# Moving the down biases to a late place and adding the last expert's last down row straight to the tokens' sums

## The reference

```python
def moe_ffn(h, w_router, b_router, w_gu, b_gu, w_down, b_down):
    logits = (h @ w_router).astype(jnp.float32) + b_router.astype(jnp.float32)
    top_v, top_i = lax.top_k(logits, TOP_K)
    gates = jax.nn.softmax(top_v, axis=-1)
    ...
    def expert_block(args):
        e, toks, gw = args
        xb = h[toks]
        gu = xb @ w_gu[e] + b_gu[e]
        gate = jnp.minimum(gu[:, :D_FF], SWIGLU_LIMIT)
        up = jnp.clip(gu[:, D_FF:], -SWIGLU_LIMIT, SWIGLU_LIMIT)
        act = gate * jax.nn.sigmoid(gate * SWIGLU_ALPHA) * (up + 1.0)
        y = act @ w_down[e] + b_down[e]
        return (y * gw[:, None]).astype(h.dtype)
    ...
    return jax.ops.segment_sum(y.reshape(n_slots, -1), slot_tok, num_segments=T)
```

## Time and profile before

| | |
|---|---|
| median of 3 runs | 989.25 us |
| profiled execution | 988.7 us |
| its span, first to last instruction | 986.9 us |
| PE busy | 946.6 us (96%) |
| DVE, ACT busy | 202.9 us (21%), 127.7 us (13%) |
| moved by DMA | 418.27 MB, mean 424 GB/s |

### The profile page before, as it was taken

The page is one execution under the profiler, slowest core; times in us unless marked ns, Lnnn a source line. Parts: engine busy times, 40 slices in busy tenths (PEclk is TensorE's granted clock), DMA queues, the critical chain, the costliest instruction groups (busy, mean ns, idle before and its releaser), DMA issues.

```text
span 986.9 us, 11112 instructions
## 1 busy us (share of the span) xinstructions
PE 946.6 (96%) x4508; PEld 382.4 (39%) x4508; DVE 202.9 (21%) x610; ACT 127.7 (13%) x346; POOL 14.0 (1%) x9
## 2 busy tenths in 40 slices
PE   9999999999999899898989989889989999999997
PEld 5545433333333334333333333333333333333432
DVE  4645121212111121210112121011212112111121
ACT  2433111011110111010011101001101110011101
POOL 0031000000000000000000000000000000000000
PEclk9999999999999999999999999999999999999999
DMA  9999999999999999999999999999999999999996
GB/s 374 426 423 398 412 429 434 432 430 428 432 431 429 436 430 430 434 432 429 434 433 426 437 432 428 437 430 429 436 429 431 432 429 430 431 433 430 422 422 272
DMA packets 23869, 418.27 MB, mean 424 GB/s; under 512 B 2912, under 2 KB 3296, under 8 KB 8224
## 3 DMA queue, kind: packets, MB, share of 16 engines
q1 hardware_dynamic: 23408, 417.20, 99.2%
q10 hardware_dynamic: 432, 0.66, 0.2%
HBM read 416.80 MB, written 1.05 MB: 423 GB/s over the span
## 4 chain that ended last, share of the span: by engine, by line
PE 63%; DMA 36%; DVE 1%; issue 0%; ACT 0%; SPq 0%; DVEq 0%
DMA ring<-w_gu_dram 33%; PE ps L1237 29%; PE ps L1342 14%; PE ps L1205 4%; PE ps L1189 4%; DMA ring<-w_down_dram 3%; PE ps L1066 3%; PE ps L997 2%; PE ps L1004 1%; PE ps L1293 1%; PE ps L1301 1%; PE ps L1013 0%; PE ps L1039 0%; PE ps L1058 0%; PE ps L1046 0%
## 5 line engine op out<-in xcount | busy, mean ns | idle before, releaser
L1237 PE MATMUL ps<-ring,passing 128*64 128x512 f32 x1008 | 229.1, 604 | 14.8 <-DMA ring<-w_gu_dram 14.8
L1237 PE MATMUL ps<-ring,PR 128*64 128x512 f32 x976 | 224.5, 608 | 16.4 <-DMA ring<-w_gu_dram 16.2
L1342 PE MATMUL ps<-ring,PT 128*64 128x512 f32 x984 | 218.3, 595 | 0.5 <-DMA ring<-w_down_dram 0.5
L952 DVE TENSOR_SCALAR xw<-ps 128x256 f32<-128x256 f32 x64 | 27.2, 425 | 650.0 <-PE ps L1237 650.0
L1237 PEld LDWEIGHTS ps<-ring,passing 128*64 128x64 f32 x1008 | 76.8, 139 | 158.3 <-issue 143.8
L1237 PEld LDWEIGHTS ps<-ring,PR 128*64 128x64 f32 x976 | 74.9, 140 | 157.0 <-issue 145.4
L1342 PEld LDWEIGHTS ps<-ring,PT 128*64 128x64 f32 x984 | 68.1, 137 | 129.6 <-issue 127.5
L652 ACT ACTIVATE xw<-xw 128x256 f32<-128x256 f32 x64 | 26.6, 416 | 484.5 <-DVE xw L952 484.5
L1205 PE MATMUL ps<-PT 64*128 64x512 f32 x248 | 69.7, 640 | 0.0
L1189 PEld LDWEIGHTS ps<-qk,X 128*128 128x128 f32 x512 | 59.6, 191 | 18.8 <-issue 18.8
L1189 PE MATMUL ps<-qk,X 128*128 128x128 f32 x512 | 65.7, 281 | 0.0
(11 more groups left out here) (198 smaller groups left out, 374.6 us busy)
## 6 DMA issues: line engine op xcount, KB each, us to landing
ring<-w_gu_dram SPq DMA_DIRECT2D x48, 4096.0 KB, 28.2
ring<-w_down_dram SPq DMA_DIRECT2D x25, 4096.0 KB, 29.7
ring<-w_gu_dram SPq DMA_DIRECT2D x14, 2048.0 KB, 14.2
ring<-w_gu_dram SPq DMA_DIRECT2D x6, 3072.0 KB, 23.2
ring<-w_down_dram SPq DMA_DIRECT2D x5, 2048.0 KB, 23.1
ring<-w_gu_dram SPq DMA_DIRECT2D x9, 1024.0 KB, 9.6
ring<-w_down_dram SPq DMA_DIRECT2D x8, 1024.0 KB, 25.9
ring<-w_down_dram SPq DMA_DIRECT2D x2, 3584.0 KB, 27.6
```

The source lines that it names most:

```text
L952: nc.vector.tensor_scalar(gb[:, b, :], gu[:, b, 0, :], LIMIT, None, ALU.min).then_inc(g_ready, 1)
L1237: last = mm(ps[64 * j:64 * j + 64, GU + b, :], lhs, halves[j][:, 512 * b:512 * b + 512], start=start, stop=stop)
L1342: last = mm(ps[64 * j:64 * j + 64, bank, :], at[:, k, 64 * (c - GU_PIECES):64 * (c - GU_PIECES) + 64], rows[:, 512 * j:512 * j + 512], sta ...
```

## The change

1. **Biases late, half a row early.** Where `b_down` was loaded, the first half (512 of 1024 columns) of the first down row of expert 26 is now loaded into the same place, `PT[:, 1, 512:1024]`. The ring load of that expert's down weights leaves it out. `b_down` is stored twice over on the host side (128 partitions in place of 64) and is loaded into `spare`, whose weights expert 24 has used by then, in SyncE's order behind the first gate-up pair of expert 26. The four bias products stand behind expert 27 in place of expert 3.
2. **The last down row.** Down row 7 of expert 31 no longer goes through `ye`. PE makes `a_tokens` ahead of time: the activations that belong to this row, turned to the tokens with the gates (128 features x 256 tokens). ScalarE copies it to SBUF. When row 7 is there, four direct products over 128 rows add `a_tokens` times the row to the sums. Between them stand the four 64-row products that bring rows 0 to 6 to the tokens.
3. **Order at the end.** `to_tokens(0)` of expert 30 stands ahead of rows 0 and 1, `to_tokens(1)` ahead of row 2.
4. **Stores.** Four stores of 256 KB, each issued after its copy (SyncE for the first half of a tile, ScalarE for the second), in place of one of 512 KB and two of 256 KB.

```diff
-        "b_down": np.asarray(inputs["b_down"]).reshape(NE, 2, DM // 2).transpose(1, 0, 2).reshape(2 * NE, DM // 2),
+        "b_down": np.tile(np.asarray(inputs["b_down"]).reshape(NE, 2, DM // 2).transpose(1, 0, 2).reshape(2 * NE, DM // 2), (2, 1)),
...
-        aT_last, ye_last = gb.rearrange("p b (f s) -> p (b f) s", f=2), sg.rearrange("p b n -> p (b n)")
+        aT_last, ye_last = extra[:, 0, 0:512].rearrange("p (f s) -> p f s", f=4), sg.rearrange("p b n -> p (b n)")
+        a_tokens = extra[:, 1, 0:T * P]
...
-        down_ahead = [mixP[:, :, :].rearrange("p g s -> p (g s)"), xT[:, FF:2 * FF]]
+        down_ahead = [mixP[:, :, :].rearrange("p g s -> p (g s)"), xT[:, FF:2 * FF], PT[:, 1, 512:1024]]
+        DOWN_AHEAD = (DM, DM, DM // 2)
+        bdn = spare[:, 0:512]
...
             sp.wait_ge(half_used, 1)
-            sp.dma_start(bdn, b_down).then_inc(ld_bdn, 16)
+            load_down_ahead(2)
...
-                load_pair(s, NE - 3 * TURN, 2 * FF if gu_ahead else DM if s in (TP + GU_PIECES, TP + PIECES + GU_PIECES) else 0)
+                u, c = (s - TP) // PIECES, (s - TP) % PIECES
+                down_part = DOWN_AHEAD[u] if s > TP and u < len(DOWN_AHEAD) and c == GU_PIECES else 0
+                load_pair(s, NE - 3 * TURN, 2 * FF if gu_ahead else down_part)
+                if s == TP + 2 * PIECES:
+                    sp.dma_start(bdn, b_down).then_inc(ld_bdn, 16)
...
-            sp.wait_ge(out_v, 1)
-            sp.wait_ge(out_a, 1)
-            sp.dma_start(out_t[0], X[:, 0, :]).then_inc(stored, 16)
-            sp.wait_ge(out_v, T)
-            sp.dma_start(out_t[1][:, 0:512], X[:, 1, 0:512]).then_inc(stored, 16)
-            sp.wait_ge(stored, 16 * 3)
+            for t in range(T):
+                sp.wait_ge(out_v, t + 1)
+                sp.dma_start(out_t[t][:, 0:512], X[:, t, 0:512]).then_inc(stored, 16)
+            sp.wait_ge(stored, 16 * 2 * T)
...
-            down_out(NE - 1, 0, GU + 1, ye_last)
+            act.wait_ge(a_tokens_psum, 1)
+            nc.scalar.copy(a_tokens, ps[:, GAT, T * P:2 * T * P]).then_inc(a_tokens_sb, 1)
+            act.wait_ge(last_rows, 1)
+            nc.scalar.copy(ye_last, ps[:, GU + 1, :]).then_inc(y_sb, 1)
...
                 act.wait_ge(acc_final, 2 * t + 2)
                 nc.scalar.copy(X[:, t, 512:1024], ps[:, ACC[t] + 1, :]).then_inc(out_a, 1)
-            act.wait_ge(out_a, T)
-            act.dma_start(out_t[T - 1][:, 512:1024], X[:, T - 1, 512:1024]).then_inc(stored, 16)
+                act.wait_ge(out_a, t + 1)
+                act.dma_start(out_t[t][:, 512:1024], X[:, t, 512:1024]).then_inc(stored, 16)
...
-                dve.wait_ge(acc_final, 2 * t + 2)
+                dve.wait_ge(acc_final, 2 * t + 1)
                 nc.vector.tensor_copy(X[:, t, 0:512], ps[:, ACC[t], :]).then_inc(out_v, 1)
...
-            down_last(aT_last, GU + 1, range(2))
-            pe.wait_ge(gt_sb, NE - 1)
+            pe.wait_ge(gt_sb, NE)
+            mm(ps[:, GAT, T * P:2 * T * P], gb[64:128, 1, P:2 * P], GT_last[64:128].rearrange("p t s -> p (t s)"), start=True, stop=True, skip_group_check=True).then_inc(a_tokens_psum, 1)
             pe.wait_ge(y_sb, NE - 1)
             to_tokens(0)
-            down_last(aT_last, GU + 1, range(2, KC))
+            down_last(aT_last, GU + 1, range(2))
             to_tokens(1)
-            pe.wait_ge(gt_sb, NE)
-            pe.wait_ge(y_sb, NE)
+            down_last(aT_last, GU + 1, range(2, KC - 1))
+            pe.wait_ge(a_tokens_sb, 1)
+            row = last_row()
             for t in range(T):
-                for last in to_tokens(t, GT_last, ye_last):
-                    last.then_inc(acc_final, 1)
+                for j in range(2):
+                    direct = mm(ps[:, ACC[t] + j, :], a_tokens[:, t * P:(t + 1) * P], row[:, 512 * j:512 * j + 512], start=False, stop=True, skip_group_check=True)
+                    if t == T - 1 and j == 1:
+                        direct.then_inc(pieces_used, 1)
+                    if t == 0 and j == 0:
+                        pe.wait_ge(y_sb, NE)
+                    mm(ps[:, ACC[t] + j, :], GT_last[64 * j:64 * j + 64, t, :], ye_last[64 * j:64 * j + 64, :], start=False, stop=True, skip_group_check=True).then_inc(acc_final, 1)
```

More of the change, by code:

```diff
@@ L206, in layer_kernel @@
         pooled = PT[:, 1, :].rearrange("p (g s) -> p g s", g=NG)
-        bdn = PT[0:2 * NE, 1, 512:1024]
         tmp = PR[:, 1, :]
@@ L308, in layer_kernel @@
         ld_wout, ld_bdn, ld_bgu = sem("ld_wout"), sem("ld_bdn"), sem("ld_bgu")
-        ld_down_ahead = [sem(f"ld_down_ahead{u}") for u in range(2)]
+        ld_down_ahead = [sem(f"ld_down_ahead{u}") for u in range(3)]
         landed = [sem(f"landed{c}") for c in range(RING // 2)]
@@ L342, in layer_kernel @@
         more_done = sem("more_done")
+        a_tokens_psum, a_tokens_sb, last_rows = sem("a_tokens_psum"), sem("a_tokens_sb"), sem("last_rows")
         acc_final, out_a, out_v = sem("acc_final"), sem("out_a"), sem("out_v")
@@ L416, in load_down_ahead @@
             def load_down_ahead(u):
-                sp.dma_start(down_ahead[u], w_dn_k[:, NE - 2 * TURN + u, 0:DM]).then_inc(ld_down_ahead[u], 16)
+                sp.dma_start(down_ahead[u], w_dn_k[:, NE - 2 * TURN + u, 0:DOWN_AHEAD[u]]).then_inc(ld_down_ahead[u], 16)
             def load_aside(k):
@@ L1331, in down @@
                         first_ahead = early in (0, 1) and c == GU_PIECES
+                        half_ahead = early == 2 and c == GU_PIECES and k == 0
                         rows = piece(c, 4)[:, k, :]
@@ L1340, in down @@
                             wait_landed(c)
+                        if half_ahead:
+                            pe.wait_ge(ld_down_ahead[2], 16)
                         for j in range(2):
                             last = mm(ps[64 * j:64 * j + 64, bank, :], at[:, k, 64 * (c - GU_PIECES):64 * (c - GU_PIECES) + 64],
-                                      rows[:, 512 * j:512 * j + 512],
-                                      start=c == GU_PIECES and k == 0, stop=c == PIECES - 1 and k == 3)
-                        if k == 3:
+                                      down_ahead[2] if half_ahead and j == 0 else rows[:, 512 * j:512 * j + 512],
+                                      start=c == GU_PIECES and k == 0, stop=c == PIECES - 1 and k == (2 if step == "last" else 3))
+                        if step == "last" and c == PIECES - 1 and k == 2:
+                            last.then_inc(last_rows, 1)
+                        elif k == 3:
                             last.then_inc(pieces_used, 1)
@@ L1348, in down, with last_row @@
                             last.then_inc(row_used, 1)
+                def last_row():
+                    pe.wait_ge(landed_end[u, GU_PIECES, KC - 1], 16)
+                    return piece(PIECES - 1, 4)[:, 3, :]
                 if last_two:
-                    return gate_up, between, turn_round, turn_gates, down
+                    return gate_up, between, turn_round, turn_gates, down, last_row
                 if step == "more":
@@ L1372, in _ @@
                 expert(0, u, "first" if u == 0 else None)
+            with pe.Fori(1, TURNS - 2) as r:
+                for u in range(TURN):
+                    expert(r, u)
+            for u in range(TURN):
+                expert(TURNS - 2, u, early=u)
             pe.wait_ge(ld_bdn, 16)
@@ L1378, in _ @@
                     mm(ps[:, ACC[t] + c, :], GdT[c * NE:(c + 1) * NE, t, :], bdn[c * NE:(c + 1) * NE, :], start=False, stop=True, skip_group_check=True)
-            with pe.Fori(1, TURNS - 2) as r:
-                for u in range(TURN):
-                    expert(r, u)
-            for u in range(TURN):
-                expert(TURNS - 2, u, early=u)
             for u in range(TURN - 2):
                 expert(TURNS - 1, u, early=TURN + u)
-            gate_up, between, _, _, down = expert(TURNS - 1, TURN - 2, "last but one")
+            gate_up, between, _, _, down, _ = expert(TURNS - 1, TURN - 2, "last but one")
             gate_up()
             between()
-            gate_up, _, turn_round, turn_gates, down_last = expert(TURNS - 1, TURN - 1, "last")
+            gate_up, _, turn_round, turn_gates, down_last, last_row = expert(TURNS - 1, TURN - 1, "last")
             gate_up()
```

## The result

The change makes the kernel slower: 993.01 us (991.93 to 993.93, 6 runs) against 989.25 us (988.49 to 990.02, 6 runs) in the same comparison, a ratio of 1.0039 (95% interval 1.0028 to 1.0049). A second comparison of the two gave 1.0031 (1.0020 to 1.0041), with a median of 992.24. The forecast was 994.1 us in a range of 991.8 to 996.2. The profiled execution took 992.06 us with a span of 990.3 us, 3.4 more than the 986.9 of the earlier trace rows; the forecast was 5.0 more.

The account below looks back on a forecast made before the run. Stream and PE bound the end, after 978.5 us PE alone. Row 6 ending at 979.8, plus 6.9 and 1.4, gives 988.1; copy and store end at 991.9, 5.0 over the span: 994.25, stated as 994.1, range 991.8 to 996.2.

Parts of the forecast that it names:

- What bounds the kernel: End of kernel: bound twice, by the weight stream and by PE, and after 978.5 us by PE alone.
- Part 3: PE's tail after row 6: eight products at 0.86 each, 6.9 us, plus eight changes of shape, 1.4 us.
- Rival B: PE's tail: lone 64-row products run in the shadow of full ones, so not slower, 989.3 us; chance 0.06.
- rival A: Late biases and PE's tail: no lateness from biases, changes of shape free, 992.0 us; chance 0.11.
- Part 1: Late biases: about 0.4 us on the stream, and PE 0.9 late at the end of expert 30's down.
- the recovery: PE's waits after 875 us, before the one at 970.9: 0.9 + 0.5 = 1.4 us absorbs late bias products.
- The late 0.05: Weight stream, late: biases come in and 256 KB of weights leave a 4 MB transfer, costing 0.05 us.
- The early 0.33: Weight stream, early: 256 KB of weights replace 128 KB of biases, costing 0.33 us; lower bound for the stream 0.
- The 0.27: to_tokens(0) at the end: 0.27 us from the copy's end to the product, so it starts at 971.5.
- Part 4: Stores at the end: the last store goes alone and lands 2.5 us after issue, bounds 1.9 and 3.0.
- C: Stream and tail: short loads slow the stream by 1.5 us, changes cost 0.34 each, 996.1 us; chance 0.07.
- D: Last down row: still waited for, landing at 979.7; result within 0.4 of the forecast and counted there.

Follow-up runs that it names:

- e3: Changed kernel with every 64-row product at the end run over all 128 rows (sums differ from the reference): 990.88 us, ratio 1.0016 to the kernel before.
- e1: Changed kernel with the four direct products first, then the 64-row products in two pairs: 991.56 us, ratio 1.0024 to the kernel before.
- e2: Changed kernel ordered by token tile, two direct products and one pair of 64-row products each: 990.55 us, ratio 1.0015 to the kernel before.
- e5: Kernel before with only the late biases and the early half row of expert 26: 989.09 us against 989.0.
- e6: Changed kernel without the late biases and the early half row: 992.33 us against 989.0 for the kernel before.
- e7: Kernel before with only the four stores and the earlier copy on VectorE: 989.25 us against 989.0.
- e8: Kernel before with only to_tokens(0) of expert 30 moved ahead of rows 0 and 1 of expert 31: 989.14 us against 989.0.
- e10: Kernel before without the code for further passes, which this input skips: 988.73 us against 989.03.
- e9: e1 without the code for further passes, which this input skips: 991.06 us against 989.03 for the kernel before.
- e4: The changed kernel unaltered, run again: 992.24 us against 989.10 for the kernel before, ratio 1.0031.
- e11: Changed kernel without the four 64-row products at the end, so rows 0 to 6 never reach the tokens: 989.28 us against 989.03 before.

## Why the prediction was right, and where it was off

**What bounds the kernel.** Right. The end is what lies behind row 6: the time from there to the last landing, less the 8.0 of before, tells the difference of the medians within 0.7 us in every run with a direct row (7.9: 0.25; 9.6: 1.45 and 2.0; 9.9: 1.8; 10.3: 2.0; 11.1: 2.5; 11.2: 3.1, 3.3 and 3.8). The wait for `ye_last` and the landing of row 7, which the change takes away, were covered: PE comes to row 7 at 978.66, 0.3 after its landing, and before it came to it 0.2 to 0.3 after its landing too.

**Part 3, eight products in place of six.** Right in mechanism and size. Forecast was 8.3 from row 6's end to the last product's end; from row 6's end to the last copy it was to be 988.35 - 979.8 = 8.55, and is 987.20 - 978.66 = 8.54. The 0.86 for a lone 64-row product, taken from near the upper bound, is 0.85 (e3 with e1 and e2), and the change of shape, taken as 0.17, is 0.196. The rule of the Trainium skill, "TensorEngine Tiling (Array Packing)", Key Properties, that a change of tiling mode drains the array, agrees, since none of the changes was free: e3 takes seven of the changes away and gets 1.36 back. Rival B falls with it, and rival A as well, whose changes of shape were free.

**Part 1, the late biases: 0.9 late was wrong.** PE is 0.1 early (the copy at 969.59, before 969.72), and e5 measures the biases at nothing. The step that failed is the recovery, 1.4 us out of the waits of the earlier trace rows. A wait in a trace is counted from the modelled end of a product, which lies 0.16 behind the work (a record of 0.59 where the next starts 0.43 later). So the five small waits, 0.9 and 0.5, hid 5 x 0.16 = 0.8 more: 2.2 were there to be filled, and the 1.9 of bias products fit. The trace after bears it out, with 1.9 filled and 0.35 of waiting left in the rows from 965.54. That the bias products fitted is shown by e5; the 0.16 is worked out, not measured by itself.

**The stream.** The late 0.05 is small against what can be seen; row 7 landed 0.1 later than before. The early 0.33 was not seen: the dip to 184 GB/s of the earlier trace rows is gone with the 64-partition load, and the window at 80 us has 413 where 395 stood. The page has the same in its fourth slice of 40, some 74 to 99 us: 398 to 403 in the five profiles without the half row (before, e6, e7, e8, e10), 411 to 414 in the nine with it. The short load in that place had cost the stream something of its own, and the lower bound, 0, was the right one. Together with part 1 this set row 6's end at 979.8; it was 978.66, and this 1.1 is the larger part of the miss. A smaller reading is in it too. The 0.27 from ScalarE's copy to the product was no wait for the copy, since PE was busy with its own products then; after the change `to_tokens(0)` starts 0.05 behind the copy (969.59 + 0.59 = 970.18, and 970.23), which is 0.2 of the 1.1.

**Part 4, the stores.** The term was mis-sized: the last store alone takes 2.05, not 2.5. That is 0.45 less, and 5.0 - 1.1 - 0.45 = 3.4 is what the span shows. The spacing that PE's slow products give the stores is itself worth something: with the same four stores within 1 us, e9 needs 3.1 and e1 4.6. That is why a PE part that is 4.8 longer costs 3.2.

**Rivals.** C (the stream suffers) falls with the stream, and D (row 7 still waited for) with the timeline, where PE has no wait ahead of 978.66. A's time, 992.0, is near the second comparison's 992.24, but for another reason: its lateness of 0 was right, and its free changes of shape, which by 0.17 each were worth 1.4, were wrong.

**How much of it was luck.** The mechanism and PE's 8.5 us behind row 6 were right, and the two misses, 1.1 and 0.45, both made the forecast too long. In the span A's 2.7 is nearer to the 3.4 measured than the forecast's 5.0. The medians of the second comparison and of e6 (992.24 and 992.33) lie only 0.4 and 0.5 above the lower bound of the range; that the first, 993.01, lies nearer its middle is the scatter between comparisons.

## What to carry to other kernels

Count products at the end by what they do to the array: two half-size products that share it cost one, and one put alone between full ones costs a full one and two changes of shape. Taking away a wait for the last transfer pays only if work remains that is shorter than what it displaces; here PE came to the last row after the row had landed, so nothing could be won. Before a wait is counted as spare time, add what the modelled end of the product ahead of it hides (0.16 here), and before stores are counted, ask how many are issued within one store's length.

## What was not expected of the hardware

A change between 128 x 128 and 64 x 128 products cost 0.196 us, with the same 1.054 of spacing in e4 and e6, and the lone 64-row product saved nothing that could pay for it (0.85 against 0.858). With 128 rows in place of 64 the same eight products reached the last copy 1.36 us sooner (7 x 0.196, e3 beside the change).

A store of 256 KB alone landed 2.0 to 2.1 us after its issue, and the same store 3.1 behind three others (e9, where no instructions are read at the end). In the kernels that read a packet of 16 KB of instructions among the last stores, a store took 3.8 and 4.0 (e4 and after, the same one), 4.6 (e1) and 3.6 (e11), but 2.7 in e3 and, where the packet was read before the store's own data moved, 2.1 in e6. What the packet costs in the median stays open, since e9 gained 0.5 with intervals that overlap.

A load of 128 KB on 64 partitions held the stream up more than one of 256 KB on 128 partitions in the same place: 395 to 400 GB/s from 80 to 100 us in five profiles with the first, 413 to 414 in nine with the second.
